# Delta rule's triangular inverses: five levels in 32x32 blocks instead of 64x64

## The chip, the cores and the metric

The kernel runs on one core of one Trainium2 chip. The metric is the device time of one execution in microseconds (us); lower is better. The engines are PE (TensorE: a weight load, PEld, and a matmul that streams the other operand past the loaded weights), DVE (VectorE), ACT (ScalarE), POOL (GpSimd) and SP (SyncE). PE reads SBUF and writes PSUM; DVE and ACT carry PSUM back to SBUF.

## The reference

One DiT-like block with a bidirectional gated delta rule, followed by two layers of a hybrid block (retention, RG-LRU, forgetting attention, MLP). 256 tokens, width 1024, float32. The change is in one part of the first block: the unit lower triangular system of each chunk of the delta rule.

```python
a_mat = jnp.where(strict, jnp.einsum('nbhid,nbhjd->nbhij', kb, kc) * decay, 0.0)
eye = jnp.eye(CHUNK, dtype=f32)
t_inv = lax.linalg.triangular_solve(eye + a_mat, jnp.broadcast_to(eye, a_mat.shape),
                                    left_side=True, lower=True, unit_diagonal=True)
u_val = jnp.einsum('nbhij,nbhjd->nbhid', t_inv, vb)
w_key = jnp.einsum('nbhij,nbhjd->nbhid', t_inv, kb * jnp.exp(gc)[..., None])
```

It runs for 4 heads, over 256 context tokens and 256 tokens of x, once forward and once backward. The kernel works in chunks of 128 tokens: 4 chunks ("tiles" g) x 4 heads x 2 directions = 32 inverses of 128x128 triangular matrices.

## The kernel before

The program runs in stages on all engines, ordered by semaphores that are written out by hand: each `wait_ge` holds the engine that issues it, in its own program order. Weights stream through a ring of `raw` buffers loaded by SP (`raw<-stream`), ACT rounds them to `w_hi` and DVE makes the remainder `w_lo`; PE multiplies three products per tile (L335 to L337). The modulation matrix is loaded by POOL in pieces of 1 MB into two buffers (`ada_raw<-ada`, L325) and multiplied by `ada_mm` (L460), pieces of which are placed between other work.

The delta rule's stage for direction d (0 and 1, one after the other) first builds the matrices `Bm` (L579 to L585 on PE, L1636 to L1653 on DVE), tile by tile. Then comes the inverse, all 16 matrices of a direction side by side. It is a block doubling: at level `lvl` the inverses `T` of diagonal blocks of size 2^lvl are joined in pairs to blocks of twice the size; level 6 joins the two 64x64 halves. Before, levels 0 to 5 treat each 128x128 matrix as two 64x64 blocks on the diagonal (r = 0 and r = 64), each held at its own rows of a tile with 64 columns per head: `Tm` (the inverse), `Uc` (its transpose), `X` (scratch). PSUM bank 4+g holds tile g. A level from 1 to 5 has three steps of PE, each 4 tiles x 4 heads x 2 blocks = 32 matmuls, one wait per tile:

- X (L617): `Bm` block times `Tm`; DVE multiplies the result with the level's mask into `X` (L1696, semaphore inv_x).
- T (L629): `Uc` times half of the columns of `X`; DVE subtracts it from `Tm` (L1701, inv_t).
- transpose (L636): `Tm` times the identity; ACT copies the result to `Uc` (L1102, inv_u), at level 5 to the two diagonal 64x64 blocks of `U` (L1104, L1105), 8 copies.

The next level's X waits for inv_u. Level 0 has the X step alone; DVE makes `Tm` (L1678, L1679) and, from `Bm` directly, `Uc` (L1673, L1680); it also sets the empty corner of `U` to zero (L1671). After the X step of level 0 PE does one `ada_mm` (32 matmul records; in direction 1 also an `ada_tr`, L471). Level 6 is 16 matmuls for X (L602), DVE's copy (L1685), 16 matmuls (L608) and DVE's copy into the off-diagonal block of `U` (L1688). Then the next direction begins, or, after direction 1, the scan: DVE clears the state (L1704, L1705) and PE starts at L649.

In the trace every float32 matmul shows as two weight loads and two matmuls (a step of 32 matmuls is "x64" on PEld and "x64" on PE). The stage is written out in full, without a loop, and queue q8 of the DMA list carries instructions.

Of the kernel before, what the change touches and what calls it, by code (L numbers as in the profile page):

```python
# [16 lines left out]
P = 128  # L17
D = 1024
KT = D // P
T = 256  # L20
# [8 lines left out]
HEADS = 4  # L29
# [61 lines left out]
def build_program(nc, io, layers=LAYERS):  # L91
# [6 lines left out]
    with ctx:  # L98
# [116 lines left out]
        Bm = at("Bm", [P, 4, 4, P], A[0])  # L215
        Tm = at("Tm", [P, 4, 4, 64], A[6])
        Uc = at("U_blocks", [P, 4, 4, 64], A[6] + 4096)
        identc = rstd[:, 0:64]
        X = at("X", [P, 4, 4, 64], F[3])
        dec = at("dec", [P, 2, 4, P], F[3])  # L220
# [110 lines left out]
        def _(pe):  # L331
# [240 lines left out]
            for d in range(2):  # L572
# [19 lines left out]
                for lvl in range(7):  # L592
                    size = 1 << lvl
                    pcol, rcol = (0, 1) if d == 0 else (1, 0)
                    def half(ap, which):
                        return ap.rearrange("p (g two s) -> p g two s", two=2, s=size)[:, :, which, :]
                    if lvl == 6:
                        lo, hi = (0, 64) if d == 0 else (64, 0)
                        for g in range(4):
                            pe.wait_ge(S("inv_u"), d * 28 + 20 + g + 1)  # L600
                            for h in range(HEADS):
                                last = mm(ps[hi:hi + 64, 4 + g, h * 64:(h + 1) * 64], Bm[lo:lo + 64, g, h, hi:hi + 64],  # L602
                                          Tm[lo:lo + 64, g, h, :], start=True, stop=True)
                            last.then_inc(S("inv_x_mm"), 1)
                        for g in range(4):
                            pe.wait_ge(S("inv_x"), d * 24 + 20 + g + 1)
                            for h in range(HEADS):
                                last = mm(ps[lo:lo + 64, 4 + g, 256 + h * 64:256 + (h + 1) * 64], X[hi:hi + 64, g, h, :],  # L608
                                          U[hi:hi + 64, d, g, h, hi:hi + 64], start=True, stop=True)
                            last.then_inc(S("inv_u_mm"), 1)  # L610
                        continue
                    for g in range(4):
                        if lvl > 0:
                            pe.wait_ge(S("inv_u"), d * 28 + (lvl - 1) * 4 + g + 1)
                        for h in range(HEADS):
                            for r in (0, 64):
                                last = mm(ps[r:r + 64, 4 + g, h * 64:(h + 1) * 64], Bm[r:r + 64, g, h, r:r + 64],  # L617
                                          ident[r:r + 64, r:r + 64] if lvl == 0 else Tm[r:r + 64, g, h, :], start=True, stop=True)
                        last.then_inc(S("inv_x_mm"), 1)
                    if lvl == 0:  # L620
                        if d == 1:
                            ada_tr(2)
                        ada_mm(16 + 4 * d)
                        continue
                    for g in range(4):
                        pe.wait_ge(S("inv_x"), d * 24 + (lvl - 1) * 4 + g + 1)
                        for h in range(HEADS):
                            for r in (0, 64):
                                last = mm(ps[r:r + 64, 4 + g, h * 32:(h + 1) * 32], Uc[r:r + 64, g, h, :],  # L629
                                          half(X[r:r + 64, g, h, :], pcol), start=True, stop=True)  # L630
                        last.then_inc(S("inv_t_mm"), 1)
                    for g in range(4):
                        pe.wait_ge(S("inv_t"), d * 20 + (lvl - 1) * 4 + g + 1)
                        for h in range(HEADS):
                            for r in (0, 64):
                                last = mm(ps[r:r + 64, 4 + g, h * 64:(h + 1) * 64], Tm[r:r + 64, g, h, :],  # L636
                                          ident[r:r + 64, r:r + 64], start=True, stop=True)
                        last.then_inc(S("inv_tr"), 1)
# [292 lines left out]
        def _(act):  # L931
# [160 lines left out]
            for e in range(8):  # L1092
                act.wait_ge(S("dec_min"), e + 1)
                act_(dec[:, e % 2, :, :], dec[:, e % 2, :, :], ACT.Exp).then_inc(S("dec_exp"), 1)
                if e == 7:
                    ada_rows(2)
                    ada_out(2)
                if e % 4 == 3:
                    for i in range(20):
                        act.wait_ge(S("inv_tr"), e // 4 * 20 + i + 1)  # L1100
                        if i < 16:
                            act_(flat(Uc[:, i % 4, :, :]), ps[:, 4 + i % 4, 0:T], ACT.Copy).then_inc(S("inv_u"), 1)  # L1102
                        else:
                            act_(U[0:64, e // 4, i % 4, :, 0:64], ps[0:64, 4 + i % 4, 0:T].rearrange("p (h n) -> p h n", h=4), ACT.Copy)  # L1104
                            act_(U[64:P, e // 4, i % 4, :, 64:P], ps[64:P, 4 + i % 4, 0:T].rearrange("p (h n) -> p h n", h=4), ACT.Copy)\  # L1105
                                .then_inc(S("inv_u"), 1)
            for b in (3, 4):
# [286 lines left out]
        def _(dve):  # L1394
# [222 lines left out]
            tt(q3, q3, bc(sm[:, 5, 16:24], P), ALU.mult).then_inc(S("kq_norm"), 1)  # L1617
            lvl_masks = cu[:, A_LVL:A_LVL + 14 * P].rearrange("p (l n) -> p l n", l=14)
            order(tt(lvl_masks[:, :, 0:64], lvl_masks[:, :, 0:64], lvl_masks[:, :, 64:P], ALU.add))
            order(tt(identc, ident[:, 0:64], ident[:, 64:P], ALU.add))  # L1620

# [33 lines left out]
            for d in range(2):  # L1655
                mat_decay(d, 0)
                for t in range(4):
                    if t < 3:
                        mat_decay(d, t + 1)
                    mat_tile(d, t)  # L1660
                lo, hi = (0, 64) if d == 0 else (64, 0)
                for lvl in range(7):
                    size = 1 << lvl
                    pcol = 0 if d == 0 else 1
                    level = lambda dd: cu[:, A_LVL + (dd * 7 + lvl) * P:A_LVL + (dd * 7 + lvl) * P + 64]

                    def half(ap, which):
                        return ap.rearrange("p h (g two s) -> p h g two s", two=2, s=size)[:, :, :, which, :]
                    if lvl == 0:
                        dve.wait_ge(S("mat_ev"), 4 * (d + 1))  # L1670
                        order.mark(nc.vector.memset(U[hi:hi + 64, d, :, :, lo:lo + 64], 0.0))  # L1671
                        for r in (0, 64):
                            order.mark(tt(Uc[r:r + 64, :, :, :].rearrange("p g h n -> p (g h) n"),  # L1673
                                          Bm[r:r + 64, :, :, r:r + 64].rearrange("p g h n -> p (g h) n"),
                                          bmid(level(1 - d)[r:r + 64, :], 16), ALU.mult))
                        for g in range(4):
                            dve.wait_ge(S("inv_x_mm"), d * 28 + g + 1)
                            order(tt(Tm[:, g, :, :], ps[:, 4 + g, 0:T].rearrange("p (h n) -> p h n", h=4), bmid(level(d), 4), ALU.mult))  # L1678
                            order.mark(tt(Tm[:, g, :, :], bmid(identc, 4), Tm[:, g, :, :], ALU.subtract))  # L1679
                            tt(Uc[:, g, :, :], bmid(identc, 4), Uc[:, g, :, :], ALU.subtract).then_inc(S("inv_u"), 1)  # L1680
                        continue
                    if lvl == 6:
                        for g in range(4):
                            dve.wait_ge(S("inv_x_mm"), d * 28 + 24 + g + 1)
                            nc.vector.tensor_copy(flat(X[hi:hi + 64, g, :, :]), ps[hi:hi + 64, 4 + g, 0:T]).then_inc(S("inv_x"), 1)  # L1685
                        for g in range(4):
# [4 lines left out]
                    for g in range(4):  # L1691
                        if lvl == 1:
                            dve.wait_ge(S("inv_u"), d * 28 + g + 1)
                            dve.wait_ge(S("dve_order"), order.n)
                        dve.wait_ge(S("inv_x_mm"), d * 28 + lvl * 4 + g + 1)
                        tt(X[:, g, :, :], ps[:, 4 + g, 0:T].rearrange("p (h n) -> p h n", h=4), bmid(level(d), 4), ALU.mult)\  # L1696
                            .then_inc(S("inv_x"), 1)
                    for g in range(4):
                        dve.wait_ge(S("inv_t_mm"), d * 20 + (lvl - 1) * 4 + g + 1)
                        Tg = half(Tm[:, g, :, :], pcol)  # L1700
                        tt(Tg, Tg, ps[:, 4 + g, 0:P].rearrange("p (h g s) -> p h g s", h=4, s=size), ALU.subtract)\  # L1701
                            .then_inc(S("inv_t"), 1)
# [549 lines left out]
```

## Time and profile before

| | |
|---|---|
| median of 3 runs | 1930.45 us (1929.99 to 1936.29) |
| profiled execution, its own time | 1936.8 us |
| its span | 1935.0 us |
| PE busy | 1773.3 us (92%), mean granted clock 0.956 |
| DVE busy | 1149.1 us (59%) |
| ACT busy | 788.6 us (41%) |
| inverse, direction 0 | 231.85 to 272.88 us |
| inverse, direction 1 | 300.01 to 342.92 us |

Times are microseconds unless marked ns. L617 is line 617 of the kernel. Matmuls overlap: a PE record of 218 ns is a latency, and the rate is read from how long so many records take together. PEclk is TensorE's granted clock as a share of 2.4 GHz. In the timeline, the bracket behind a row is the idle time before it and what ended it; "issue" there means that the engine waited for nothing that the profile shows. The DMA list gives for a stretch the packets that began in it, by queue; q8 and q14 carry instructions.

### The profile page before, as it was taken

The page shows a single profiled execution, that of the slowest core. Times are in us where ns is not written, and L with a number is a line of the kernel's source. Part 1 is how long each engine was busy: PE and PEld are TensorE (multiplying, and loading weights), DVE is VectorE, ACT ScalarE, POOL GpSimd, SP SyncE. Part 2 cuts the span into 40 slices and gives each one's busy share as a digit, 9 for nine tenths or more (in the row PEclk, how much of TensorE's full clock was granted, in tenths as well). Part 3 has the DMA queues.
Part 4 walks back from the last instruction along what each step waited for, and adds up shares of the span by engine and source line. Part 5 has one row for each costly group of instructions (what it writes and reads, how often), then busy time and mean ns, then how long its engine had stood idle before and what let it go on. Part 6 is the DMA issues. An engine that isn't in the chain of part 4 may idle for free.

```text
span 1935.0 us, 36021 instructions
## 1 busy us (share of the span) xinstructions
PE 1773.3 (92%) x15972; PEld 1657.3 (86%) x15972; DVE 1149.1 (59%) x1479; ACT 788.6 (41%) x966; POOL 34.2 (2%) x68
## 2 busy tenths in 40 slices
PE   5996788778999989999999999998999999999998
PEld 4784687557799979999999989997999999979997
DVE  3465556553798554546778574545554688666453
ACT  3232121013433335354575444434444476545342
POOL 0001000000000000000000000000000000000000
PEclk8898798779999999999999999999999999999999
DMA  9677423443445444434545535553534455535552
GB/s 397 247 262 283 152 84 118 174 174 127 139 170 173 155 160 157 148 132 167 173 164 194 175 131 174 196 174 105 178 131 134 162 184 175 196 109 180 191 174 88
DMA packets 45215, 329.40 MB, mean 170 GB/s; under 512 B 5008, under 2 KB 5008, under 8 KB 5392
## 3 DMA queue, kind: packets, MB, share of 16 engines
q1 hardware_dynamic: 35712, 258.63, 38.5%
q0 software_dynamic: 9216, 67.11, 9.3%
q8 instruction: 119, 1.95, 0.4%
q10 hardware_dynamic: 144, 1.51, 0.2%
q14 instruction: 24, 0.20, 0.0%
HBM read 326.18 MB, written 1.05 MB: 169 GB/s over the span
## 4 chain that ended last, share of the span: by engine, by line
PE 69%; DVE 11%; ACT 8%; issue 6%; DMA 5%; SPq 0%; ACTq 0%; DVEq 0%; POOL 0%
PE ps L335 17%; PE ps L336 16%; PE ps L337 16%; ACT w_hi L946 5%; DMA ada_raw<-ada 4%; PE ps L388 4%; PE ps L460 2%; DVE w_lo L1403 2%; PE ps L439 2%; PE ps L617 1%; DMA ada<-ada 1%; DVE rsq L2103 1%; PE ps L629 1%; DVE rstd L1441 1%; PE ps L636 1%
## 5 line engine op out<-in xcount | busy, mean ns | idle before, releaser
L1403 DVE TENSOR_TENSOR w_lo<-raw,w_hi 128x2048 fp32r<-128x2048 f32 x211 | 483.2, 2292 | 508.4 <-ACT w_hi L946 507.8
L335 PE MATMUL ps<-act_hi,w_hi 128*128 128x256 f32 x2672 | 755.6, 283 | 24.1 <-DVE act_lo L1458 9.7
L336 PE MATMUL ps<-act_lo,w_hi 128*128 128x256 f32 x2672 | 744.8, 279 | 0.0
L337 PE MATMUL ps<-act_hi,w_lo 128*128 128x256 f32 x2672 | 744.6, 279 | 0.0
L946 ACT ACTIVATE w_hi<-raw 128x2048 fp32r<-128x2048 f32 (+1 forms) x233 | 428.9, 1842 | 559.4 <-PE ps L337 558.6
L335 PEld LDWEIGHTS ps<-act_hi,w_hi 128*128 128x128 f32 x2672 | 506.4, 190 | 35.8 <-issue 21.7
L337 PEld LDWEIGHTS ps<-act_hi,w_lo 128*128 128x128 f32 x2672 | 506.9, 190 | 0.0
L336 PEld LDWEIGHTS ps<-act_lo,w_hi 128*128 128x128 f32 x2672 | 505.6, 189 | 0.9
L335 PE MATMUL ps<-mlp_hi,w_hi 128*128 128x256 f32 x512 | 146.0, 285 | 9.2 <-DVE mlp_lo L2106 9.2
L336 PE MATMUL ps<-mlp_lo,w_hi 128*128 128x256 f32 x512 | 144.4, 282 | 0.0
L337 PE MATMUL ps<-mlp_hi,w_lo 128*128 128x256 f32 x512 | 144.3, 282 | 0.0
L460 PE MATMUL ps<-ada_raw,silu_c_wide 128*32 128x256 f32 x1024 | 79.8, 452 | 43.0 <-DMA ada_raw<-ada 43.0
L335 PEld LDWEIGHTS ps<-mlp_hi,w_hi 128*128 128x128 f32 x512 | 99.1, 194 | 10.1 <-DVE mlp_lo L2106 10.0
L336 PEld LDWEIGHTS ps<-mlp_lo,w_hi 128*128 128x128 f32 x512 | 99.2, 194 | 0.2
L337 PEld LDWEIGHTS ps<-mlp_hi,w_lo 128*128 128x128 f32 x512 | 99.2, 194 | 0.0
L460 PEld LDWEIGHTS ps<-ada_raw,silu_c_wide 128*32 128x32 f32 x1024 | 31.9, 123 | 78.2 <-DMA ada_raw<-ada 55.4
L1805 DVE SCALAR_TENSOR_TENSOR gacc<-gpad,vectors,gacc 128x256 f32<-128x256 f32 x176 | 84.5, 480 | 15.8 <-ACT gacc L1148 10.6
L388 PE MATMUL ps<-h_up,raw 128*128 128x256 f32 x352 | 82.2, 386 | 1.9 <-ACT h_up L1138 1.6
L388 PEld LDWEIGHTS ps<-h_up,raw 128*128 128x128 f32 x352 | 65.4, 192 | 12.7 <-ACT h_up L1138 3.0
L335 PE MATMUL ps<-w_hi,act_hi 128*128 128x256 f32 x256 | 72.6, 284 | 0.0
L336 PE MATMUL ps<-w_lo,act_hi 128*128 128x256 f32 x256 | 71.5, 279 | 0.0
L337 PE MATMUL ps<-w_hi,act_lo 128*128 128x256 f32 x256 | 71.3, 279 | 0.0
(397 smaller groups left out, 2166.9 us busy)
## 6 DMA issues: line engine op xcount, KB each, us to landing
raw<-stream SPq DMA_DIRECT2D x233, 1024.0 KB, 4.9
ada_raw<-ada POOLq DMA_DIRECT2D x64, 1024.0 KB, 6.7
ada_f<-ada SPq DMA_DIRECT2D x4, 1024.0 KB, 14.1
ada_a<-ada SPq DMA_DIRECT2D x3, 1024.0 KB, 19.9
consts_stage<-consts_a SPq DMA_DIRECT2D x1, 1728.0 KB, 32.7
consts_stage<-consts_b ACTq DMA_DIRECT2D x1, 1472.0 KB, 6.8
x<-xT SPq DMA_DIRECT2D x1, 1024.0 KB, 7.1
xc<-ctxT SPq DMA_DIRECT2D x1, 1024.0 KB, 9.1
```

The costliest lines, as they stand in the source:

```text
L335: mm(out, ah, bh, start=first, stop=False, skip_group_check=shared)
L336: mm(out, ah, bl, start=False, stop=False, skip_group_check=shared)
L337: return mm(out, al, bh, start=False, stop=last, skip_group_check=shared)
L388: mm(ps[:, bank, 0:T], raw[:, slot, k * P:(k + 1) * P], h_up[:, k, :], start=k == 0, stop=k == KT - 1)
L439: last = mm(ps[:, 7, 0:T], omean, sq[:, b, :], start=b == 0, stop=b == KT - 1)
L460: last = mm(ps[strip:strip + 32, bank, c * T:(c + 1) * T], cs_wide[:, k, 32 - 3 * j:64 - 3 * j], ada_raw[:, c, k * T:(k + 1) * T], start=j ...
L617: last = mm(ps[r:r + 64, 4 + g, h * 64:(h + 1) * 64], Bm[r:r + 64, g, h, r:r + 64], ident[r:r + 64, r:r + 64] if lvl == 0 else Tm[r:r + 64 ...
L629: last = mm(ps[r:r + 64, 4 + g, h * 32:(h + 1) * 32], Uc[r:r + 64, g, h, :], half(X[r:r + 64, g, h, :], pcol), start=True, stop=True)
L636: last = mm(ps[r:r + 64, 4 + g, h * 64:(h + 1) * 64], Tm[r:r + 64, g, h, :], ident[r:r + 64, r:r + 64], start=True, stop=True)
L946: act_(w_hi[:, s2, o:CH], raw[:, s4, o:CH], ACT.Copy).then_inc(S("hi_ready"), 1)
L1403: tt(w_lo[:, s2, :], raw[:, s4, :], w_hi[:, s2, :].bitcast(f32), ALU.subtract).then_inc(S("lo_ready"), 1)
L1805: ins = stt(acc, src, w, acc, ALU.mult, ALU.add)
```

## The change

- `Tm`, `Uc`, `X` now hold 32 columns per head, and levels 0 to 4 work on four 32x32 blocks on the diagonal (r = 0, 32, 64, 96), so on four places of the array instead of two. A step is 4 tiles x 4 heads x 4 blocks = 64 matmuls. A new tile `T64` holds the 64x64 inverses that level 6 reads, `X64` is its scratch.
- Level 0 now makes `Uc` by the same transpose step as the other levels; DVE no longer computes it from `Bm`. DVE does two operations per tile in level 0 instead of three.
- Level 5 works on off-diagonal 32x32 blocks alone: X (32 matmuls), then 48 matmuls, of which 16 give the missing block of `T64` (DVE, inv_t_off) and 32 the missing blocks of `U` (ACT). ACT copies the four diagonal 32x32 blocks from `Uc` into `U` (one copy for each block of rows) ahead of that, and DVE copies two from `Tm` into `T64`.
- `U` as a whole and `T64` are cleared once, ahead of the stage; the masks are folded to 32 columns by two reductions instead of an addition.
- Level 6 reads `T64` and `X64`, and waits for inv_t_off as well.

The core of the diff (PE, ACT, DVE in this order):

```diff
+                    if lvl == 5:
+                        for g in range(4):
+                            pe.wait_ge(S("inv_u"), d * 28 + 16 + g + 1)
+                            for h in range(HEADS):
+                                for r in (0, 64):
+                                    lo, hi = (r, r + 32) if d == 0 else (r + 32, r)
+                                    last = mm(ps[hi:hi + 32, 4 + g, h * 32:(h + 1) * 32], Bm[lo:lo + 32, g, h, hi:hi + 32],
+                                              Tm[lo:lo + 32, g, h, :], start=True, stop=True)
+                            last.then_inc(S("inv_x_mm"), 1)
+                        for g in range(4):
+                            pe.wait_ge(S("inv_x"), d * 24 + 16 + g + 1)
+                            for h in range(HEADS):
+                                for r in (0, 64):
+                                    lo, hi = (r, r + 32) if d == 0 else (r + 32, r)
+                                    if r == 64 * d:
+                                        mm(ps[hi:hi + 32, 4 + g, P + h * 32:P + (h + 1) * 32], Uc[hi:hi + 32, g, h, :],
+                                           X[hi:hi + 32, g, h, :], start=True, stop=True)
+                                    last = mm(ps[lo:lo + 32, 4 + g, 256 + h * 32:256 + (h + 1) * 32], X[hi:hi + 32, g, h, :],
+                                              Uc[hi:hi + 32, g, h, :], start=True, stop=True)
+                            last.then_inc(S("inv_o_mm"), 1)
+                        continue
...
                         for h in range(HEADS):
-                            for r in (0, 64):
-                                last = mm(ps[r:r + 64, 4 + g, h * 64:(h + 1) * 64], Bm[r:r + 64, g, h, r:r + 64],
-                                          ident[r:r + 64, r:r + 64] if lvl == 0 else Tm[r:r + 64, g, h, :], start=True, stop=True)
+                            for r in range(0, P, 32):
+                                last = mm(ps[r:r + 32, 4 + g, h * 32:(h + 1) * 32], Bm[r:r + 32, g, h, r:r + 32],
+                                          ident[r:r + 32, r:r + 32] if lvl == 0 else Tm[r:r + 32, g, h, :], start=True, stop=True)
                         last.then_inc(S("inv_x_mm"), 1)
...
+                        act_(flat(Uc[:, i % 4, :, :]), ps[:, 4 + i % 4, 0:P], ACT.Copy).then_inc(S("inv_u"), 1)
+                    act.wait_ge(S("inv_u"), e // 4 * 28 + 20)
+                    for r in range(0, P, 32):
+                        act_(U[r:r + 32, e // 4, :, :, r:r + 32].rearrange("p g h n -> p (g h) n"),
+                             Uc[r:r + 32, :, :, :].rearrange("p g h n -> p (g h) n"), ACT.Copy)
+                    for g in range(4):
+                        act.wait_ge(S("inv_o_mm"), e // 4 * 4 + g + 1)
+                        for r in (0, 64):
+                            lo, hi = (r, r + 32) if e < 4 else (r + 32, r)
+                            ins = act_(U[lo:lo + 32, e // 4, g, :, hi:hi + 32],
+                                       ps[lo:lo + 32, 4 + g, 256:384].rearrange("p (h n) -> p h n", h=4), ACT.Copy, scale=-1.0)
+                        ins.then_inc(S("inv_u"), 1)
...
+            order(nc.vector.memset(U[:, :, :, :, :], 0.0))
+            order(nc.vector.memset(T64[:, :, :, :], 0.0))
...
-                        order.mark(nc.vector.memset(U[hi:hi + 64, d, :, :, lo:lo + 64], 0.0))
-                        for r in (0, 64):
-                            order.mark(tt(Uc[r:r + 64, :, :, :].rearrange("p g h n -> p (g h) n"),
-                                          Bm[r:r + 64, :, :, r:r + 64].rearrange("p g h n -> p (g h) n"),
-                                          bmid(level(1 - d)[r:r + 64, :], 16), ALU.mult))
                         for g in range(4):
                             dve.wait_ge(S("inv_x_mm"), d * 28 + g + 1)
-                            order(tt(Tm[:, g, :, :], ps[:, 4 + g, 0:T].rearrange("p (h n) -> p h n", h=4), bmid(level(d), 4), ALU.mult))
-                            order.mark(tt(Tm[:, g, :, :], bmid(identc, 4), Tm[:, g, :, :], ALU.subtract))
-                            tt(Uc[:, g, :, :], bmid(identc, 4), Uc[:, g, :, :], ALU.subtract).then_inc(S("inv_u"), 1)
+                            order(tt(Tm[:, g, :, :], ps[:, 4 + g, 0:P].rearrange("p (h n) -> p h n", h=4), bmid(mask, 4), ALU.mult))
+                            tt(Tm[:, g, :, :], bmid(sel[:, :], 4), Tm[:, g, :, :], ALU.subtract).then_inc(S("inv_t"), 1)
```

The T step and the transpose step change in the same way as the X step (r in steps of 32, 32 columns per head).

## Rows read from the trace of the kernel before

**Rows 1.** The page's part 4: what the chain that ended last is made of.
```profile
PE 69%; DVE 11%; ACT 8%; issue 6%; DMA 5%; SPq 0%; ACTq 0%; DVEq 0%; POOL 0%
```

**Rows 2.** Stretches (busy us and records per engine, PEclk, DMA share): both directions, then parts.
```profile
231.85:272.88 41.03, 38.93 (x1121) 36.50 (x1121) 24.90 (x63) 9.18 (x24) 1.06 (x2) 0.93 0.17 62
300.01:342.92 42.91, 41.41 (x1128) 38.46 (x1128) 25.14 (x64) 9.38 (x25) 1.06 (x2) 0.90 0.17 61
246.33:264.28 17.95, 17.95 (x623) 17.95 (x620) 9.61 (x27) 4.61 (x12) 0.00 (x0) 1.00 0.02 5
240.00:244.50 4.50, 4.17 (x135) 4.04 (x136) 2.51 (x9) 1.10 (x3) 0.00 (x0) 1.00 0.98 408
310.00:315.00 5.00, 4.49 (x154) 4.35 (x151) 2.56 (x8) 0.72 (x2) 0.00 (x0) 1.00 0.91 357
```

**Rows 3.** The chain that ended last: level 0 of direction 0, then one later level.
```profile
231.85 3.68 PE ps L617 x64
235.53 2.70 PE ps L460 x32
...
256.96 1.87 PE ps L617 x64
258.82 1.84 PE ps L629 x64
260.67 1.89 PE ps L636 x64
```

**Rows 4.** Groups of instructions between 229 and 345 us, by line.
```profile
L617 PE MATMUL ps<-consts_common,Bm 64*64 64x64 f32 x128 | 7.4, 313 | 9.5 <-DVE Bm L1653 9.5
...
L1696 DVE TENSOR_TENSOR X<-ps,consts_stage 128x256 f32<-128x256 f32 x40 | 16.7, 423 | 21.3 <-PE ps L617 20.2
L1102 ACT ACTIVATE U_blocks<-ps 128x256 f32<-128x256 f32 x32 | 12.3, 385 | 51.8 <-PE ps L636 50.0
L1701 DVE TENSOR_TENSOR Tm<-Tm,ps 128x128 f32<-128x128 f32 x40 | 11.5, 288 | 5.5 <-PE ps L629 5.4
L1104 ACT ACTIVATE U<-ps 64x256 f32<-64x256 f32 x8 | 3.0, 377 | 7.8 <-PE ps L636 7.6
```

**Rows 5.** Timeline of PE alone: level 1 of direction 0, then of direction 1.
```profile
242.53 1.82 PE L636 MATMUL ps<-consts_common,Tm 64*64 64x64 f32 x55
245.30 0.45 PE L636 MATMUL ps<-consts_common,Tm 64*64 64x64 f32 x9 [0.95 <-issue]
...
312.73 1.12 PE L636 MATMUL ps<-consts_common,Tm 64*64 64x64 f32 x31
314.36 0.85 PE L636 MATMUL ps<-consts_common,Tm 64*64 64x64 f32 x22 [0.51 <-issue]
```

**Rows 6.** DMA list, stretches 246.33:264.28, 242.86:242.87, 246.32:246.33, 312.10:312.11, 315.45:315.46, in this order.
```profile
q8 instruction: 5, 0.08, 1.8%
...
q8 instruction: 1, 0.02, 561.9%
...
q8 instruction: 1, 0.02, 720.6%
...
q8 instruction: 1, 0.02, 583.8%
...
q8 instruction: 1, 0.02, 596.2%
```

**Rows 7.** DMA list of 234.07:242.86: no q8 row, this queue alone, and its issues.
```profile
q0 software_dynamic: 187, 1.40, 43.4%
issues: line engine op xcount, KB each, median us to landing
ada_raw<-ada POOLq DMA_DIRECT2D x2, 1024.0 KB, 6.5
```

**Rows 8.** One line's weight loads of 32 columns (ns min/median/max), four column strips in turn.
```profile
L460 PEld LDWEIGHTS ps<-ada_raw,silu_c_wide x1024: 105/110/178, 42.6 to 493.3; 128*32 128x32 f32 x171
```

**Rows 9.** Timeline of all engines, after DVE's work ahead of the stage, and ACT rows used as prices.
```profile
192.51 1.08 DVE L1619 TENSOR_TENSOR consts_stage<-consts_stage 128x896 f32<-128x896 f32 x1
...
196.35 0.60 ACT L1087 ACTIVATE kT<-ps 128x512 f32<-128x512 f32 x1 [0.26 <-PE ps L555]
...
198.05 0.19 ACT L1025 ACTIVATE mod_raw<-ps 128x20 f32<-128x20 f32 x1
...
201.62 0.22 DVE L1623 COPY smalls<-ps 128x64 f32<-128x64 f32 x1 [7.76 <-PE ps L565]
...
235.88 0.20 PEld L460 LDWEIGHTS ps<-ada_raw,silu_c_wide 128*32 128x32 f32 x4 [0.23 <-issue]
```

**Rows 10.** Timeline of all engines: the end of direction 1 and the scan's start.
```profile
340.52 0.42 DVE L1685 COPY X<-ps 64x256 f32<-64x256 f32 x1 [0.38 <-PE ps L602]
340.97 1.67 DVE L1688 TENSOR_SCALAR U<-ps 64x256 f32<-64x256 f32 x4
342.92 0.91 DVE L1704 MEMSET state<- 128x1024 f32 x1 [0.28 <-DVE U L1688]
```

**Rows 11.** Timeline of all engines: level 6's X for one tile, direction 0.
```profile
269.21 0.54 PEld L602 LDWEIGHTS ps<-Tm,Bm 64*64 64x64 f32 x8 [0.26 <-ACT U L1105]
```

More of the change, by code:

```diff
@@ L215, in build_program @@
         Bm = at("Bm", [P, 4, 4, P], A[0])
[L216 to L219, printed above, removed]
+        Tm = at("Tm", [P, 4, 4, 32], A[6])
+        Uc = at("U_blocks", [P, 4, 4, 32], A[6] + 2048)
+        T64 = at("T_half", [P, 4, 4, 64], A[6] + 4096)
+        X = at("X", [P, 4, 4, 32], F[3])
+        X64 = at("X_half", [P, 4, 4, 64], F[3] + 2048)
         dec = at("dec", [P, 2, 4, P], F[3])
@@ L599, in _ @@
                         for g in range(4):
+                            pe.wait_ge(S("inv_t_off"), d * 4 + g + 1)
                             pe.wait_ge(S("inv_u"), d * 28 + 20 + g + 1)
@@ L602, in _ @@
                                 last = mm(ps[hi:hi + 64, 4 + g, h * 64:(h + 1) * 64], Bm[lo:lo + 64, g, h, hi:hi + 64],
-                                          Tm[lo:lo + 64, g, h, :], start=True, stop=True)
+                                          T64[lo:lo + 64, g, h, :], start=True, stop=True)
                             last.then_inc(S("inv_x_mm"), 1)
@@ L607, in _ @@
                             for h in range(HEADS):
-                                last = mm(ps[lo:lo + 64, 4 + g, 256 + h * 64:256 + (h + 1) * 64], X[hi:hi + 64, g, h, :],
+                                last = mm(ps[lo:lo + 64, 4 + g, 256 + h * 64:256 + (h + 1) * 64], X64[hi:hi + 64, g, h, :],
                                           U[hi:hi + 64, d, g, h, hi:hi + 64], start=True, stop=True)
@@ L615, in _ @@
                         for h in range(HEADS):
-                            for r in (0, 64):
-                                last = mm(ps[r:r + 64, 4 + g, h * 64:(h + 1) * 64], Bm[r:r + 64, g, h, r:r + 64],
-                                          ident[r:r + 64, r:r + 64] if lvl == 0 else Tm[r:r + 64, g, h, :], start=True, stop=True)
+                            for r in range(0, P, 32):
+                                last = mm(ps[r:r + 32, 4 + g, h * 32:(h + 1) * 32], Bm[r:r + 32, g, h, r:r + 32],
+                                          ident[r:r + 32, r:r + 32] if lvl == 0 else Tm[r:r + 32, g, h, :], start=True, stop=True)
                         last.then_inc(S("inv_x_mm"), 1)
+                    for g in range(4 if lvl > 0 else 0):
+                        pe.wait_ge(S("inv_x"), d * 24 + (lvl - 1) * 4 + g + 1)
+                        for h in range(HEADS):
+                            for r in range(0, P, 32):
+                                last = mm(ps[r:r + 32, 4 + g, h * 16:(h + 1) * 16], Uc[r:r + 32, g, h, :],
+                                          half(X[r:r + 32, g, h, :], pcol), start=True, stop=True)
+                        last.then_inc(S("inv_t_mm"), 1)
                     if lvl == 0:
@@ L623, in _ @@
                         ada_mm(16 + 4 * d)
-                        continue
                     for g in range(4):
-                        pe.wait_ge(S("inv_x"), d * 24 + (lvl - 1) * 4 + g + 1)
+                        pe.wait_ge(S("inv_t"), d * 20 + lvl * 4 + g + 1)
                         for h in range(HEADS):
-                            for r in (0, 64):
[L629 to L637, printed above, removed]
+                            for r in range(0, P, 32):
+                                last = mm(ps[r:r + 32, 4 + g, h * 32:(h + 1) * 32], Tm[r:r + 32, g, h, :],
+                                          ident[r:r + 32, r:r + 32], start=True, stop=True)
                         last.then_inc(S("inv_tr"), 1)
@@ L1100, in _ @@
                         act.wait_ge(S("inv_tr"), e // 4 * 20 + i + 1)
[L1101 to L1106, printed above, removed]
+                        act_(flat(Uc[:, i % 4, :, :]), ps[:, 4 + i % 4, 0:P], ACT.Copy).then_inc(S("inv_u"), 1)
+                    act.wait_ge(S("inv_u"), e // 4 * 28 + 20)
+                    for r in range(0, P, 32):
+                        act_(U[r:r + 32, e // 4, :, :, r:r + 32].rearrange("p g h n -> p (g h) n"),
[7 more added lines that the diff above has]
+                        ins.then_inc(S("inv_u"), 1)
             for b in (3, 4):
@@ L1617, in _ @@
             tt(q3, q3, bc(sm[:, 5, 16:24], P), ALU.mult).then_inc(S("kq_norm"), 1)
-            lvl_masks = cu[:, A_LVL:A_LVL + 14 * P].rearrange("p (l n) -> p l n", l=14)
-            order(tt(lvl_masks[:, :, 0:64], lvl_masks[:, :, 0:64], lvl_masks[:, :, 64:P], ALU.add))
-            order(tt(identc, ident[:, 0:64], ident[:, 64:P], ALU.add))
+            masks32 = [t[:, 0:160] for t in (rstd, std)]
+            for d in range(2):
+                o = A_LVL + d * 7 * P
+                order(red(masks32[d].rearrange("p (l r) -> p l r", l=5), cu[:, o:o + 5 * P].rearrange("p (l s r) -> p l r s", l=5, s=4),
+                          AX, ALU.add))
+            order(nc.vector.memset(U[:, :, :, :, :], 0.0))
+            order(nc.vector.memset(T64[:, :, :, :], 0.0))
             dve.wait_ge(S("gc_mm"), 1)
@@ L1661, in _ @@
                 lo, hi = (0, 64) if d == 0 else (64, 0)
+                lo5, hi5 = (0, 32) if d == 0 else (32, 0)
                 for lvl in range(7):
@@ L1664, in _ @@
                     pcol = 0 if d == 0 else 1
-                    level = lambda dd: cu[:, A_LVL + (dd * 7 + lvl) * P:A_LVL + (dd * 7 + lvl) * P + 64]
+                    mask = masks32[d][:, lvl * 32:(lvl + 1) * 32] if lvl < 5 else None
                     def half(ap, which):
```

25 lines of the change are left out of this document (17 added, 8 removed).

## The prediction

> **What bounds the kernel now.** I read the page's chain first: PE holds 69% of it [rows 1], so a stage's worth is what it costs PE's program. The change touches 83.9 us of 1935.0: the inverse of direction 0 (41.0 us) and of direction 1 (42.9 us) [rows 2]. Both lie wholly on the chain. In a level of either direction PE is never idle: X, T and transpose follow each other in 1.87, 1.84 and 1.89 us, 64 records each, 5.6 us per level [rows 3]. DVE needs 4 x 0.423 + 4 x 0.288 = 2.8 us per level and ACT 4 x 0.385 = 1.5 us [rows 4]; both wait for PE. So PE's rate bounds the stage, and two rates have to be told apart.
>
> The array's rate: 64 records on two places of the array in 1.87 us is 58 ns for a pair. T streams 32 columns where X streams 64 and takes as long, so the weight load of 64 columns sets it. At 1.2 GHz (level 0's X, 3.68 us) it is 115 ns for a pair [rows 3]: it goes with the clock, as array work does.
>
> The program's rate: between 246.33 and 264.28 PE ran 623 + 620 records [rows 2] while queue q8 began 5 packets [rows 6], one per 249 records and 3.59 us. A packet is 16 KB (0.08 MB for 5) and holds PE's next instructions; the few that are missing from 256 are waits. In all of this stage PE stood still twice in the middle of a tile's matmuls, for which no semaphore can be the reason: 0.95 us up to 245.30, and 0.51 us up to 314.36, "issue" both times [rows 5]. The packet that was due had begun late, at 242.86, none having begun since 234.07 [rows 6, 7]; so also 312.10 in direction 1. In both cases `ada_raw` filled the DMA engines (share 0.98 and 0.91) [rows 2]. PE went on 2.44 and 2.26 us after the packet's start, and the next packet began 1.02 and 1.09 us after PE had gone on [rows 5, 6]. I read this as: PE's program is fetched 256 instructions at a time, one packet ahead, the next asked for when PE enters the one before it; asking to start is 1.0 us, start to use is up to 2.4 us. One such cycle is then about 3.4 us; PE eats a packet in 3.6 us, so it is hidden by a hair.
>
> **The change part by part.**
> Steps of levels 0 to 4. A float32 matmul is four instructions (two loads, two matmuls). A step was 32 matmuls, 128 instructions and 4 waits; it is now 64 matmuls, 256 instructions and 4 waits. Steps per direction: X five times, T four times, transpose five times (level 0 gets one), 14 steps, 3640 instructions, where levels 0 to 5 were 16 steps and 2112 instructions. With `ada_mm` (64 and 2 waits) it is 3706, or 14.5 packets of 256.
>
> What 64 matmuls cost is not in the trace. From below, the array's rate: four places at once, and a load of 32 columns instead of 64, thus half of the 53 ns that 128 cycles of 2.4 GHz are, plus the same 5 ns over it: 31 ns for four records, 128 records in 1.0 us against 1.87. That starts follow closely enough is shown: four loads on four strips span 0.20 us of which one takes up to 0.178, so they start some 7 ns apart [rows 8, 9]. From above, a price per record whatever its place: 29 ns each, 3.7 us. The fetch lies between: 260 instructions are 1.02 packets a step.
>
> The packet's cycle L is bounded below by 1.02 us and the packet's own 0.90 us (561.9% of 16 engines' 0.01 us [rows 6]), 1.9 us, and above by 1.02 + 2.44 = 3.46 us. I take 3.2 us: the only two whole cycles that the trace shows are 3.46 and 3.35 us, but they were taken under full DMA engines, and part of the 2.4 us may be that. The packet itself took no longer there (0.90 us) than in quiet (1.15 us for the one at 246.32), so I stay near the upper end.
>
> Sum for a direction. The first packet boundary comes early and the one behind it is in hand (PE waits 4.7 us for DVE ahead of each direction [rows 4]), so I count 14.3 cycles for levels 0 to 4: 14.3 x 3.2 = 45.8 us, and 1.2 us ahead of the first boundary. After `ada_mm` POOL loads two pieces of 1 MB, which keep the DMA engines full for about 4.5 us and put a packet off by some 2 us, as before; before, 0.95 us of it showed, now all of it does: 2.0 us (0 to 4). Under this bound, level 0's relief on DVE is worth nothing: the 2 copies of 1.2 us, the `Uc` operations and the clearing that go lie beside the fetch.
>
> Levels 5 and 6: 32 + 48 + 32 matmuls are 320 + 128 instructions and 20 waits, 1.8 packets, 5.9 us at L. Beside it runs a chain on ACT: the last `Uc` copy 0.3, four copies of 32 x 512 elements at 0.60 each as for 128x512 [rows 9] = 2.4, eight of 32 x 128, between 0.19 for 20 elements and 0.377 for 256 [rows 4, 9], at 0.28 = 2.2; then level 6 for the last tile: 8 records on one place 0.5 [rows 11], out of PE 0.2, DVE copy 0.42, again 0.5 and 0.2, DVE 0.42 [rows 10] = 2.2; with handing over 0.6 in all, 7.7 us (7 to 9). DVE's two copies into `T64` (0.7 each at most) lie beside ACT's four. The wait on inv_t_off ahead of level 6 holds PE's X; inv_u from ACT ends later, since DVE has 1.4 + 4 x 0.28 us to do where ACT has 4.6.
>
> A direction: 1.2 + 45.8 + 2.0 + 7.7 = 56.7 us; two are 113.4, and against 83.9 that is +29.5 us. `ada_tr` in direction 1 (1.8 us on PE) fits under a fetch.
>
> Ahead of the stage, DVE clears `U` (4096 elements, four times the 0.91 us of 1024 [rows 10]), `T64` (0.91) and reduces 2 x 640 elements (0.9 each), with handing over 1.2 us: 7.6 us from 192.5, where 1.3 us of work stood. DVE then waits 7.76 us for PE until 201.62 [rows 9]; it ends at 200.1. Cost nothing; if the reductions take twice as long it is 0.3 us late.
>
> PE would be busy for 1.1 us in each 3.2, so the granted clock may fall to 1.2 GHz; a step takes twice 1.0 us then and still fits under L. I add nothing.
>
> Sum: 1936.8 + 29.5 = 1966.3 for the profiled execution; the median of the runs shown is 6.3 us under it, so 1960.
>
> **The rivals.**
> Faster (17%): packets come more than one ahead, and the array's rate holds. Then level 0 is X at 1.2 GHz 1.8, `ada_mm` 2.7 and the transpose 1.0 with DVE's 0.6 between: 6.1 us; levels 1 to 4 are 3.0 us of PE and 0.3 at the turns, 13.2 us; levels 5 and 6 are 7.7: 27.0 us, in direction 1 28.8. That saves 28 us: 1902. For it: only two stalls, 1.46 us in all, are seen, and the whole argument on packets rests on them. Against it: their position in mid tile, and that 1.02 and 1.09, 2.44 and 2.26 agree. The fetch must let a packet go every 2.2 us for the time to stay as it was, and every 1.0 us for this rival.
> The Trainium skill speaks for this rival: the page "Runtime: NRT & Kernel Launch", section "Instruction fetch mechanics", gives PE room for 2048 instructions, refilled in blocks of 256, says the next block is fetched while the current one runs, and that fetching hides behind about 20 sequencer cycles per instruction. The blocks of 256 agree with rows 2 and 6. The 20 cycles do not: four instructions per 58 ns are 14.4 ns each, less than the 16.7 ns that 20 cycles at 1.2 GHz would be, an estimate from that page.
>
> A price per record (10%, slower too): 29 ns per record, wherever it goes. A step is 3.7 us, 14 of them 51.8; with `ada_mm` 2.7, and 7.7, 62.2 per direction, 1.8 more in direction 1: +42 us, 1973. For it: a pair of 32 columns in T takes as long as one of 64. Against: in level 0 the same pair takes 115 ns at half the clock, and level 6, on one place alone, needs 58 ns per record (8 loads in 0.54 us, the last of them 0.13) where two places need 29 [rows 11].
> The Trainium skill's page "TensorE: Matmul & The Clock Gate", section "Back-to-back issue gap", has about 25 ns per matmul for 1 to 64 columns; by that a step would be 3.2 us and the kernel at about 1960, an estimate from the page. Rows 3 do not settle it.
>
> A short cycle (6%): L is 1.9 to 2.4 us, close to the packet alone. At 2.1 the sum is 2 x (1.2 + 30.0 + 2.0 + 7.7) = 81.8, 2 us less than before: 1928, no change.
>
> **How the numbers follow.** Forecast 67% (L from 2.5 to 3.6: at 3.6 and 4 us of contention 2 x 64.4 - 83.9 = +45; at 2.5, +9.5), price per record 10%, short cycle 6%, array's rate 17%. Slower by over 0.3% (5.8 us, about what a measurement of this kernel can tell from no change): 67 + 10, less 1 for a cycle just over the bound: 76%. Within 0.3%: 6%. Faster: 18%. The range leaves out the array's rate (17%) and 3% at the top: from 1930, the upper part of the short cycle, to 1974.
>
> **What would show it.** Right: in the new trace PE stands still "issue" in mid tile about once per step; q8 packets in the stage come about 3.2 us apart, 16 or 17 per direction instead of 9; between stalls a step's 128 records take 1.0 us at 2.4 GHz or under 2 at 1.2; the clock in the stage is under the 0.93 and 0.90 of before. Wrong: packets nearer than 2.1 us, or levels of 3.3 us without "issue", speak for the array's rate; records evenly 25 to 29 ns apart with no stalls speak for the price per record. If levels 5 and 6 take over 9 us, ACT's copies were priced too low. Outside 190 to 345 us nothing should move.

## The result and the profile after

| | before | after |
|---|---|---|
| median of the runs, us | 1933.13 (1929.99 to 1936.29, 4 runs) | 1987.30 (1984.90 to 1989.31, 4 runs) |
| profiled execution, its span, us | 1935.0 | 1983.1 |
| inverse of direction 0, us | 41.03 [rows 2] | 66.26 |
| inverse of direction 1, us | 42.91 [rows 2] | 65.38 |
| instruction packets on q8 | 119 | 133 |

The change makes the kernel slower: ratio 1.0280, 95% interval 1.0255 to 1.0305. The direction was forecast, the size was not: 1960 with a range up to 1974. The profiled execution took 1984.9 us where the sum gave 1966.3, a miss of 18.6 us. The other 8.7 of the 27.3 us between the medians is the step from profiled execution to median: the prediction took off 6.3 us, as in the runs before, but the changed kernel's median lies 2.4 us above its profiled execution.

Page of the changed kernel, the instruction queue of part 3 (packets, MB, share of 16 engines) and part 4 (answers to rows 1):

```profile
q8 instruction: 133, 2.18, 0.4%
...
PE 67%; DVE 11%; issue 8%; ACT 8%; DMA 5%; SPq 0%; ACTq 0%; DVEq 0%; POOL 0%
```

Stretches of the changed kernel (answer to rows 2; columns: busy us and records of PE, PEld, DVE, ACT, POOL, then PEclk, DMA share, GB/s): both directions, levels 1 to 4 of direction 0, and levels 5 and 6 of each direction.

```profile
232.50:298.76 66.26, 39.36 (x2049) 35.42 (x2049) 16.59 (x58) 10.21 (x32) 1.05 (x2) 0.55 0.11 39
327.61:392.99 65.38, 42.06 (x2056) 37.88 (x2056) 16.55 (x58) 10.41 (x33) 1.06 (x2) 0.53 0.11 40
247.10:287.40 40.30, 21.32 (x1425) 20.00 (x1425) 7.33 (x29) 4.17 (x15) 0.00 (x0) 0.50 0.02 4
287.46:298.76 11.30, 10.11 (x229) 9.77 (x219) 6.33 (x18) 4.92 (x13) 0.00 (x0) 0.50 0.01 3
381.00:392.99 11.99, 10.17 (x222) 9.72 (x216) 6.29 (x18) 4.94 (x13) 0.00 (x0) 0.50 0.01 3
```

PE, which filled 38.93 of 41.03 us in rows 2, is now idle for 26.9 of 66.26 us, and the granted clock is 0.50, that is 1.2 GHz, from the restart in level 1 at 247.17 to the end of level 6. The chain says what PE waited for. Chain of the changed kernel, direction 0 (start, length, what; answer to rows 3):

```profile
232.50 1.93 PE ps L640 x128
...
239.02 0.57 issue
239.59 0.27 PE ps L658 x9
...
240.94 6.22 issue
247.17 0.33 PE ps L640 x9
247.50 1.57 PE ps L647 x119
249.07 1.56 issue
250.63 0.31 PE ps L647 x9
250.94 1.62 PE ps L658 x119
252.56 1.81 issue
254.37 0.33 PE ps L658 x9
...
258.11 0.34 PE ps L640 x9
...
287.18 0.28 PE ps L658 x5
```

From the first step of level 1 on, every step of direction 0 (L640 is X, L647 T, L658 the transpose) stops after 119 of its 128 records, in the middle of a tile, where no semaphore is waited for. From one restart to the next PE runs 9 + 119 matmul records with as many loads: 256 instructions, one packet of 16 KB. So the four waits of a step take no place of their own in the packet; the prediction had counted 260 instructions for a step. The restarts are 3.46 or 3.74 us apart (247.17, 250.63, 254.37, 258.11). The DMA list of the changed kernel, stretches 244.80:244.81, 248.21:248.22, 251.66:251.67 and 255.49:255.50, has the packets between them:

```profile
q8 instruction: 1, 0.02, 601.2%
...
q8 instruction: 1, 0.02, 547.5%
...
q8 instruction: 1, 0.02, 738.1%
...
q8 instruction: 1, 0.02, 799.4%
```

PE goes on 2.37, 2.41, 2.70 and 2.62 us after such a start, and the next packet starts 1.05, 1.04 and 1.12 us after PE has gone on. Those are the two parts from which the prediction built its cycle [rows 5, 6], now once per step. The 6.22 us at 240.94 belong to a packet that began only at 244.80, where by the same pattern it was asked for at 239.59, when PE went on; in between queue q8 carried none (DMA list of 239.60:244.80):

```profile
q0 software_dynamic: 219, 1.60, 78.6%
```

### The profile page after: what moved, and what is told of

The parts are those of the page before. It is cut to its first block, busy times and chain, and to the rows that moved or that the text cites. A ratio compares the mean times of both kernels' runs of the same rounds, so it can differ in the third digit from the quotient of the medians.

```text
span 1983.1 us, 39743 instructions
## 1 busy us (share of the span) xinstructions
PE 1776.5 (90%) x17828; PEld 1658.3 (84%) x17828; DVE 1137.8 (57%) x1471; ACT 790.4 (40%) x982; POOL 34.3 (2%) x68
## 3 DMA queue, kind: packets, MB, share of 16 engines
HBM read 326.18 MB, written 1.05 MB: 165 GB/s over the span
## 4 chain that ended last, share of the span: by engine, by line
PE 67%; DVE 11%; issue 8%; ACT 8%; DMA 5%; SPq 0%; ACTq 0%; DVEq 0%; POOL 0%
PE ps L336 16%; PE ps L338 16%; PE ps L337 16%; ACT w_hi L968 5%; DMA ada_raw<-ada 4%; PE ps L389 4%; PE ps L461 2%; DVE w_lo L1431 2%; PE ps L440 1%; DMA ada<-ada 1%; DVE rsq L2140 1%; PE ps L658 1%; PE ps L640 1%; DVE rstd L1469 1%; PE ps L647 1%
## 5 line engine op out<-in xcount | busy, mean ns | idle before, releaser
L1842 DVE SCALAR_TENSOR_TENSOR gacc<-gpad,vectors,gacc 128x256 f32<-128x256 f32 x176 | 84.4, 480 | 15.9 <-ACT gacc L1176 10.7
## 6 DMA issues: line engine op xcount, KB each, us to landing
ada_f<-ada SPq DMA_DIRECT2D x4, 1024.0 KB, 14.6
```

What stands on the lines that cost most here:

```text
L1842: ins = stt(acc, src, w, acc, ALU.mult, ALU.add)
```

## The experiments

**Is it the array or the instructions?** The first kernel doubles the array's streaming in the X steps of levels 1 to 4 and leaves the instruction count alone.

```diff
-last = mm(ps[r:r + 32, 4 + g, h * 32:(h + 1) * 32], Bm[r:r + 32, g, h, r:r + 32], Tm[r:r + 32, g, h, :], ...)
+last = mm(ps[r:r + 32, 4 + g, o:o + 64], Bm[r:r + 32, g, h, r:r + 32],
+          Tm[r:r + 32, g, b:b + 2, :].rearrange("p h n -> p (h n)"), ...)     # b = min(h, 2)
```

(Shortened: `...` stands for the arguments that stay. DVE reads the wide result at its new place.)

> Changed kernel with the X step of levels 1 to 4 streaming 64 columns instead of 32 (the second head's columns are junk that nobody reads, the result stays the same): same number of instructions, twice the columns in 4 of 14 steps per direction. Theory (PE waits for its program, one packet of 256 instructions per 3.46 or 3.74 us): array work is covered, so the X steps still begin 3.5 to 3.7 us after the step before them, and the kernel stays within 2 us of 1987. Rival (the array or a price per column sets the step): 32 rounds of four matmul records go from 54 to about 107 ns each at 1.2 GHz, +1.7 us per step, 8 steps, +14 us: about 2001.

Measured: 1983.87 us (1982.74 to 1989.47), ratio 1.0238 (1.0214 to 1.0262), no slower than the changed kernel. Chain of this kernel, one level of direction 1 (L643 is the wide X step):

```profile
348.80 0.95 issue
349.75 1.95 PE ps L643 x65
...
352.60 0.62 issue
353.21 1.09 PE ps L653 x66
...
355.14 1.53 issue
356.68 1.11 PE ps L664 x66
```

The X step has more work and the stalls in it and right behind it are shorter: 0.95 and 0.62 us, where the transpose, which is as narrow as before, has 1.53. Restarts still come 3.46 us apart (349.75, 353.21, 356.68 to within 0.01). The array's work lies under the fetch.

**Take the fetch away.** Levels 1 to 4 on PE become a hardware loop of four turns with one body of three steps (some 780 instructions); the array's work is that of the changed kernel, except that T streams 32 columns instead of 16. The same is done to the kernel before, levels 1 to 5, and T's width is changed by itself, unrolled, as a control.

```diff
...
+if lvl == 1:
+    with pe.Fori(0, 4) as i:
+        x_step(i * 4, d * 28)
+        t_step(i * 4, d * 24)
+        tr_step(i * 4, d * 20 + 4)
...
```

(`x_step`, `t_step` and `tr_step` hold the three steps, each wait on an instruction of its own.)

> Changed kernel with PE's levels 1 to 4 written once and run as a loop of 4 (T step streams all 32 columns so that its instructions do not depend on the level; DVE takes its half of them; waits for a register's value sit on an instruction of their own). Same matmuls, same order; 768 matmul instructions and some 40 others per turn. Theory (fetching the program bounds the stage): if a loop's body stays in PE's instruction store, turns 2 to 4 need no packets, a level falls from 10.9 us to 3.3 to 4.5 us, and the stage of a direction from 66 and 70 us to 40 to 45: kernel at 1930 to 1945. If the body does not stay, every turn fetches again and the time is that of the changed kernel or worse, 1987 to 2010, with as many q8 packets. Rival (a price per matmul record or the clock bounds the stage): the packets go but a level still takes 10 us or more.

> Kernel before with PE's levels 1 to 5 written once and run as a loop of 5 (T step streams all 64 columns; otherwise as before). 384 matmul instructions and some 40 others per turn. Theory: before, the array was the bound and only two stalls of 1.46 us in all came from the program, so at best 1.5 us is gained and the waits as own instructions cost some tenths per level: 1928 to 1940, and no idle time in mid tile. Rival (the kernel before was itself bound by its program's packets): a level falls well under 5.6 us, towards 5.0, and the kernel to 1924 or less.

> Changed kernel with the T step streaming all 32 columns and DVE taking its half, as in the run with the loop, but written out in full. Control for that run. Theory (program packets): the T step's array work is covered, so it stays within 3 us of the changed kernel, 1987. Rival (the loop run was faster for its T step and not for its loop): near 1946.

Measured: the loop in 32x32 blocks 1946.16 us (1942.56 to 1956.87), ratio 1.0058 (1.0036 to 1.0081): 9 us over its kernel before by the medians, 11 by the ratio, instead of 54. The loop in 64x64 blocks 1939.93 us, ratio 1.0013 (0.9996 to 1.0029): no gain, as there the array's rate covers the fetch. Its profiled execution is not free of idle time in mid tile, as was expected: the transpose of the first turn stands still for 2.02 us in direction 0 and 2.79 us in direction 1. The control 1979.99 us (two runs), ratio 1.0242 (1.0213 to 1.0271): T's width matters little or not at all, the loop does. Chain of the loop in 32x32 blocks, direction 0, from its first turn to its third (L642 X, L652 T, L662 transpose), and the q8 row of its DMA list for 256.2:272.0, which holds levels 2 to 4 and the start of level 5:

```profile
242.22 5.16 issue
...
249.30 1.95 issue
...
253.22 2.30 issue
...
256.21 1.96 PE ps L642 x128
258.17 1.56 PE ps L652 x127
259.73 1.48 PE ps L662 x116
...
261.60 1.56 PE ps L642 x116
263.15 1.22 PE ps L652 x92
264.38 1.22 PE ps L662 x87
...
q8 instruction: 1, 0.02, 0.4%
```

The first turn stalls once a step like the changed kernel. From the second on PE doesn't wait for instructions in mid tile, a single packet is fetched where straight code takes nine for three levels, and a level takes 5.4 us (256.21 to 261.60, mean clock 0.71), then 4.6 and 4.5 us at full clock, against 5.6 in 64x64 blocks [rows 3]. So the small blocks do help the array, by 1 us a level at full clock, in turns that are not fetched. The first turn costs far more than that: 15.4 us (240.76 to 256.21) where level 1 of the kernel before takes 7.5 (238.23 to 245.75). The directions are 46.3 and 47.5 us long against 41.0 and 42.9. Level, directions and median all end just above what was expected (4.5, 45 and 1945 us).

**The late packet after `ada_mm`.** POOL holds back one pair of pieces until level 5 of direction 0 is over; direction 1 stays as it was.

```diff
+if m == 34:
+    pool.wait_ge(S("inv_u"), 24)
```

> Changed kernel, POOL's load of piece 34 of the modulation matrix (and with it all behind it) held until level 5 of direction 0 has begun, so that no transfer runs beside levels 1 to 4 of direction 0. Theory (the stall of 6.2 us in level 1 is a packet that had to queue behind 2 MB of ada_raw): that stall falls to the 1.5 to 1.8 us of all others, direction 0 gets 4 to 5 us shorter, direction 1 stays, kernel at about 1983. Rival (the stall has another cause, such as the first pass through a level): nothing moves.

> The run with the loop (32x32 blocks, PE's levels 1 to 4 as a loop of 4) with POOL's load of piece 34 held until level 5 of direction 0 has begun. Theory: packets are still fetched in the first turn, and the one delayed behind ada_raw cost 5.2 us there against some 2 for its neighbours, so 3 to 5 us go: 1941 to 1943. Rival (the stall belongs to entering the loop): unchanged, 1946.

Chain of the changed kernel with that wait, then of the loop with it:

```profile
243.79 2.38 issue
...
240.99 2.15 issue
```

The stalls of 6.22 and 5.16 us fall to 2.38 and 2.15: the late packet was late because of POOL's two pieces. Neither falls to the 1.5 to 1.8 us that was expected. The time follows only in part. With the unrolled kernel the median is 1982.66 us (1978.85 to 1985.34), ratio 1.0228 (1.0200 to 1.0257), whose interval still touches that of the changed kernel. In its profiled execution direction 0 is 64.5 us instead of 66.3: of 3.8 us saved at this place, 2.0 came back, 0.5 in a longer first stall (1.09 instead of 0.57 us), 0.6 in a slower `ada_mm`, 0.7 in the next 11 cycles (40.7 us instead of 40.0) and 0.2 in levels 5 and 6. With the loop, direction 0 is 43.4 instead of 46.3 us but the median is 1945.42 us (1944.25 to 1950.51), against 1946.16: the expected 3 to 5 us cannot be seen. Where it went was not settled.

**Level 5 alone.** The kernel before, with only level 5 on off-diagonal blocks.

> Kernel before (64x64 blocks in levels 0 to 4, as before) with level 5 alone changed: 32 matmuls for X on the off-diagonal 32x32 blocks, then 48, of which 16 complete Tm (DVE) and 32 give the missing blocks of U (ACT); ACT copies the two 64x64 diagonals of U from Uc first. PE loses 192 + 192 records of a level that took 5.6 us and gets 160 + 160 small ones, 320 instructions where 384 were, and no longer waits for the eight copies into U, but for two copies of 64x1024 (1.0 to 1.2 us each) and eight of 32x128 (0.27 each). Theory: this half of the change has no share in the loss, since its instructions get fewer: between 2 us faster and 3 us slower than before per direction, 1931 to 1943 beside a before of 1937. Rival (the loss comes with the off-diagonal level and its copies): 5 us or more per direction, 1947 or more.

Measured: 1936.85 us (1933.63 to 1947.02), ratio 1.0013 (0.9996 to 1.0030). Levels 5 and 6 of this kernel, direction 0:

```profile
262.04:271.63 9.59, 7.87 (x224) 7.50 (x225) 5.34 (x16) 4.63 (x11) 0.00 (x0) 0.76 0.01 3
```

9.6 us, where level 5 from 262.56 and level 6 to 272.88 took 10.3 before; in direction 1 it is 10.7 (332.2 to 342.9) against 10.5. By itself that part of the change is worth nothing measurable either way. The loss comes with the five levels of 32x32 blocks: in them, and at the low clock that they leave to levels 5 and 6.

**More instructions without array work.** A dose: the kernel before with 8, and with 32, repeated waits on values already reached ahead of every tile of levels 1 to 5.

```diff
...
+for _ in range(8):     # 32 in the other kernel
+    pe.wait_ge(S("inv_t"), d * 20 + (lvl - 1) * 4 + g + 1)
```

(Ahead of the transpose; X and T have the same with their own semaphores.)

> The kernel before with eight more waits on PE ahead of each tile of levels 1 to 5, on values already reached (a satisfied wait, no array work): a step is 160 instructions instead of 128, nothing else changes. Fetch theory (256 of PE's instructions per 3.62 us, the mean cycle in the changed kernel): a step takes 160 x 14.1 ns = 2.26 us instead of 1.87, 30 steps give +12 us, 1946, with 'issue' stalls in the middle of tiles and 3 to 4 packets more on q8 (119 to 123). If the waits only cost the time in which PE's sequencer handles them and the fetch is no limit, all idle time stands at the tiles' starts, none in mid tile, and it is a quarter of what the kernel with 32 waits adds. If neither counts, 1935.

> The same with 32 more waits per tile: 256 instructions a step, as in the changed kernel, but the array work of the kernel before. Fetch theory: a step takes one cycle, 3.6 us instead of 1.87, 30 steps give +52 us, 1987, stalls in mid tile where a packet ends, 15 packets more on q8 (134). If waits cost only handling time, each of the 3840 costs the same w as in the kernel with 8 per tile, so four times its gain or loss, with no stall in mid tile. If the fetch theory is right and a wait also costs handling time (some 10 to 30 ns each, a guess), the handling lies under the fetch until it alone passes 3.6 us a step, 1.9 us of it beside 1.87 of array work.

Measured: 1956.93 us (ratio 1.0120, 1.0081 to 1.0158) and 2105.66 us (1.0868, 1.0820 to 1.0916). Chain of the kernel with 32 waits, one T step:

```profile
267.40 1.07 PE ps L633 x16
268.47 0.73 issue
269.20 1.07 PE ps L633 x16
```

Here the idle time stands between tiles, where the waits are, at 0.73 us for 32, or 23 ns each, and the granted clock is 0.50 between 255 and 275 us (1.07 us for 16 records). That is the sign of the second theory, and the handling alone is 2.9 us a step. But its sum fails: the kernel with 8 waits adds 23 us where a quarter of the other's 172 would be 43. Nor was the dose what was meant: q8 has 120 and 126 packets, 1 and 7 more than 119, not 4 and 15, so a repeated wait takes at most about half an instruction's place. The kernel with 8 waits does have idle time in mid tile, against the second theory (2.40 and 0.45 us in direction 0 between 245 and 275 us, 2.76 and several of 0.1 to 0.3 in direction 1), more than the kernel before; one cannot read a limit from it. Its steps without a stall take 2.1 to 2.3 us instead of 1.84 to 1.89, so 8 waits a tile cost 8 to 13 ns each where they can be seen. As a test of the fetch this pair failed; it shows what waits cost.

## Why the prediction was half right

**The bound.** "PE's program is fetched 256 instructions at a time, one packet ahead", read from two stalls of 1.46 us in all, was right, and so were both signs that it named: a stall in mid tile once per step, and 16 packets in each direction where 9 and 8 began before. The doubled streaming shows that the array does not set the time, the loop shows that the instructions do. The rival of the array's rate falls with that. So does the price per record: between stalls 119 records take 1.57 to 1.62 us at 1.2 GHz, 13 ns each, not 25 to 29, and they come in bursts. The short cycle of 1.9 to 2.4 us was never seen. The Trainium skill ("Runtime: NRT & Kernel Launch", "Instruction fetch mechanics") has the fetch hidden while an instruction takes about 20 cycles. PE used its packets at up to 256 in 1.9 us, 7.4 ns per instruction, and got them at 256 in 3.46 to 3.74, 13.5 to 14.6 ns per instruction. As an estimate in cycles of 1.2 GHz that is 9 used against 16 to 18 got: the latter is of the order of that page's figure, and this change is on its wrong side. What it says of 2048 instructions of room fits the loop of some 780, which stays in the store; a straight program still got only one packet ahead.

**The sizes.** All in us, per direction, against the sum of the prediction (L is the packet's cycle, from one restart to the next):

| term | predicted | direction 0 | direction 1 |
|---|---|---|---|
| start to the restart in level 1's X | 1.2 + 3.3 x 3.2 + 2.0 = 13.8 | 14.7 | 12.5 |
| the next 11 cycles | 11 x 3.2 = 35.2 | 40.0 | 39.7 |
| from there to level 4's end | 0 | 0.3 | 1.1 |
| levels 5 and 6 | 7.7 | 11.3 | 12.0 |
| together | 56.7 | 66.3 | 65.4 |

- L was taken as 3.2 us and is 3.64 and 3.61 on the mean: 4.7 us per direction, half of the miss. The failing step is "part of the 2.4 us may be that", the discount for full DMA engines. In levels 1 to 4 their share is 0.02, and the two parts are 2.4 to 2.7 and 1.0 to 1.1 us. The only two whole cycles in the trace of before, 3.46 and 3.35 us, were the better estimate; even the upper bound of 3.46 was too low for 12 of the 22 cycles (3.74 us, once 4.01).
- The packet delayed by POOL's pieces: taken at 2.0 us (0 to 4). It began 5.2 us after PE had gone on instead of 1.0, so 4.2 us late, in direction 0; in direction 1 the stall there was 2.86 us, 1.3 over the usual 1.53. The stall with the pieces held back confirms the cause for direction 0. What PE had in hand at the start lasted longer than counted (the first stall comes 6.5 us into direction 0 and 9.7 us into direction 1), which hides the miss in the first row of the table.
- Levels 5 and 6, forecast at 7.7 us (7 to 9). "If they take over 9 us, ACT's copies were priced too low" was the wrong sign: ACT's prices were right. Timeline of the changed kernel, ACT and then DVE, levels 5 and 6 of direction 0:

```profile
287.88 2.54 ACT L1126 ACTIVATE U<-U_blocks 32x512 f32<-32x512 f32 x4
290.44 2.26 ACT L1132 ACTIVATE U<-ps 32x128 f32<-32x128 f32 x8
...
295.24 0.43 DVE L1725 COPY X_half<-ps 64x256 f32<-64x256 f32 x1 [0.42 <-PE ps L625]
295.73 0.42 DVE L1728 TENSOR_SCALAR U<-ps 64x256 f32<-64x256 f32 x1
296.58 0.42 DVE L1728 TENSOR_SCALAR U<-ps 64x256 f32<-64x256 f32 x1 [0.44 <-PE ps L631]
...
298.29 0.42 DVE L1728 TENSOR_SCALAR U<-ps 64x256 f32<-64x256 f32 x1 [0.44 <-PE ps L631]
```

  ACT took 2.54 + 2.26 us where 2.4 + 2.2 stood. And ACT was not on the path. The chain of the changed kernel in level 6 of direction 0 (L625 X, L631 the second step):

```profile
291.60 3.28 PE ps L625 x29
...
295.20 3.06 PE ps L631 x29
```

  PE was at level 6's X tiles 1.1 us before ACT's last copy ended at 292.70, and from there to its last tile it had no pause of length: at 1.2 GHz PE, not ACT, sets the pace here. In level 5 the chain is on PE too, with one more stall for instructions in each direction (0.68 and 1.08 us). Counted from ACT's end, level 6 took 6.1 us (to 298.76) where 2.2 stood. The chain of the kernel before has the same work at 2.4 GHz:

```profile
269.57 0.39 ACT U L1105
...
270.68 1.70 PE ps L608 x29
...
272.41 0.43 DVE U L1688
```

  From ACT's end at 269.96 to 272.88 it is 2.9 us. So 0.7 us were miscounted: the sum took the last tile alone through both of its steps, but PE has all four X tiles ahead of the first T tile in its program, and four T tiles queue behind the last X. The other 3.2 us, by comparison with the kernel before, are the clock: a T tile takes 0.85 us now, where four took 1.70. The loop with the held-back pieces, with a mean clock of 0.83 in levels 5 and 6, lies between: 4.1 us behind ACT's end, 9.3 in all.
- The clock: "may fall to 1.2 GHz and a step ... still fits under L. I add nothing." It fell (0.50), and under L it did cost nothing. But it was still down where nothing hides PE: 3.2 us in levels 5 and 6 of each direction, and in the products behind direction 0: L580's first eight take 2.08 us instead of 1.16 and L586's 1.70 instead of 0.89. From 298.76 to 327.61 the stage between the directions is 1.7 us longer than before, for which the sum had nothing. Outside the stage, as said, little moved: direction 0 starts 0.65 us later, and what follows direction 1 is 2.0 us shorter.
- DVE's work ahead of the stage cost nothing, as said: it was done in time although the two reductions took 1.24 us each, not 0.9.

The miss of 18.6 us in the profiled execution is thus 9.6 + 8.7 in the two directions and 1.7 between them, less 1.3 in the rest. L and the tail both erred to the low side. The top of the range lay 7 us per direction above the sum. L took 4.7 of them and the tail 3.6 and 4.3; the range did not let the two err together. The steps that failed are thus two: the discount on L, and levels 5 and 6 priced along ACT at the full clock.

## What to carry to other kernels

Before cutting tiles smaller, count the engine's instructions in straight code: in this kernel straight code got 256 instructions per 3.46 to 3.74 us (once 4.01), so they arrive too late where a change leaves the engine less time than that for 256 of them; a hardware loop escapes this from its second turn on, and pays only if enough turns follow. One or two unexplained stalls in the middle of a tile are worth pricing as they are: the full cycle that they show was closer than any discount. Where PE is going to idle, price what follows it at 1.2 GHz, not only the stalled part.

## What the hardware showed that was not expected

- The restart of PE's program comes in steps: 3.46 or 3.74 us, in this kernel once 4.01, at DMA engines that are otherwise 2% busy. Nothing in the runs says why there are two lengths.
- Four 32x32 float32 records on four places of the array take 43 to 49 ns together (128 in 1.37 to 1.56 us in the loop), not the estimated 31; two of 64x64 take 58 ns [rows 3]. Quartering the blocks' area gains 1 us in 5.6 even without the fetch.
- 32 waits in a row on PE that are already satisfied cost 23 ns each, eight in a row 8 to 13 ns each; a repeated one takes at most about half an instruction in the packets.
- One packet of 16 KB can be held up for 4.2 us by 2 MB of data that POOL asked for shortly before.
